# The next head's queries and key scores: in five parts between the row sums instead of in one block

## The reference, cut to what matters

```
def peer_ffn(xm, w_query, sub_keys, expert_u, expert_v):      # blocks of 128 tokens
    def one_block(xblk):
        q = (xblk @ w_query).reshape(B, TOKEN_BLOCK, N_PEER_HEADS, 2, SUBKEY_DIM)   # 8 heads, 2 x 256
        s = jnp.einsum('bthpd,hpnd->bthpn', q, sub_keys)                            # 2 x 128 key scores
        vals, idx = lax.top_k(s, PEER_TOPK)                                         # 16 of each half
        ...                                          # 256 sums, the best 16 of them, their softmax g
        u = expert_u[eidx]
        h = jnp.einsum('btd,bthkd->bthk', xblk, u)
        act = jax.nn.gelu(h, approximate=False) * g
        return jnp.einsum('bthk,bthkd->btd', act, expert_v[eidx])
```

## Time and profile before

| | us |
|---|---|
| median of 3 runs | 3779.18 (3777.73 to 3786.63) |
| the profiled execution | 3777.06 |
| its span, from the first to the last instruction | 3775.3 |
| expert stage of the first layer, first to last gather | 298 to 1065 |
| expert stage of the second layer, first to last gather | 1342 to 2104 |

### The profile page before, as it was taken

One profiled execution on the slowest core, in us unless ns is written; L12 is line 12 of the kernel. 1 busy time (PEld: TensorE's weight loads), 2 busy tenths in 40 slices (PEclk: granted clock), 3 DMA queues, 4 the chain that ended last, 5 costly groups with the idle time before them and its releaser, 6 DMA issues. The chain is left out here.

```text
span 3775.3 us, 50620 instructions
## 1 busy us (share of the span) xinstructions
PE 3284.1 (87%) x18912; PEld 2562.1 (68%) x18912; DVE 2393.1 (63%) x4688; ACT 1438.5 (38%) x2831; POOL 1237.1 (33%) x1160
## 2 busy tenths in 40 slices
PE   6997787888779878888887799999999999999999
PEld 5883343333259843443332599888899998898899
DVE  7766655655567566666655565866565656757565
ACT  4532222222146322222221344565554444655443
POOL 1306677777723067777777200000000000000000
PEclk8999999999999999999999999999999999999999
DMA  7668999999976489999999554434355554334355
GB/s 276 228 221 335 359 368 358 374 362 339 370 290 212 148 329 369 378 369 372 370 344 358 219 183 147 146 114 138 129 174 184 179 180 140 134 125 133 129 184 162
DMA packets 258289, 937.13 MB, mean 248 GB/s; under 512 B 29312, under 2 KB 30720, under 8 KB 257792
## 3 DMA queue, kind: packets, MB, share of 16 engines
q0 software_dynamic: 161280, 587.27, 41.6%
q1 hardware_dynamic: 96768, 346.62, 27.2%
HBM read 932.73 MB, written 1.05 MB: 247 GB/s over the span
## 5 line engine op out<-in xcount | busy, mean ns | idle before, releaser
L639 PE MATMUL M<-rows,diag 128*128 128x512 f32 x2048 | 1010.1, 635 | 327.0 <-DMA rows<-in_expert_v_dram,expert 210.2
L639 PEld LDWEIGHTS M<-rows,diag 128*128 128x128 f32 x2048 | 382.6, 199 | 944.1 <-issue 501.6
L252 DVE TENSOR_TENSOR w_low<-ring,w_high 128x1024 fp32r<-128x1024 f32 x560 | 688.6, 1232 | 427.4 <-ACT w_high L244 424.5
L1118 DVE CUSTOM_DVE_ANT_0 rows<-rows,attn 128x1024 f32<-128x1024 f32 x512 | 611.5, 1224 | 337.4 <-DMA rows<-in_expert_u_dram,expert 335.6
L271 PE MATMUL G<-x_high,w_high 128*128 128x256 f32 x2576 | 761.9, 296 | 60.3 <-DVE w_low L252 27.2
L274 PE MATMUL G<-x_high,w_low 128*128 128x256 f32 x2576 | 735.4, 285 | 0.0
L244 ACT ACTIVATE w_high<-ring 128x1024 fp32r<-128x1024 f32 x560 | 588.5, 1054 | 352.1 <-PE G L271 326.7
L273 PE MATMUL G<-x_low,w_high 128*128 128x256 f32 x2448 | 700.0, 286 | 0.0
L397 POOL DMA_INDIRECT rows<-in_expert_u_dram,expert x512 | 561.5, 1097 | 392.7 <-DVE expert L1100 163.6
L397 POOL DMA_INDIRECT rows<-in_expert_v_dram,expert x512 | 579.8, 1132 | 159.9 <-issue 110.7
L271 PEld LDWEIGHTS G<-x_high,w_high 128*128 128x128 f32 x2576 | 501.6, 195 | 74.5 <-issue 48.9
(11 more groups left out here) (350 smaller groups left out, 4507.2 us busy)
## 6 DMA issues: line engine op xcount, KB each, us to landing
ring<-in_stream_dram SPq DMA_DIRECT2D x654, 512.0 KB, 3.4
ada_ring<-in_ada_stream_dram POOLq DMA_DIRECT2D x80, 512.0 KB, 4.9
rows<-in_ada_stream_dram POOLq DMA_DIRECT2D x16, 512.0 KB, 17.1
rows<-in_expert_u_dram,expert POOLq DMA_INDIRECT x512, 6.2
rows<-in_expert_v_dram,expert POOLq DMA_INDIRECT x512, 6.3
const<-in_const_dram SPq DMA_DIRECT2D x1, 1096.5 KB, 11.0
x<-in_x_dram SPq DMA_DIRECT2D x1, 1024.0 KB, 5.3
out_dram<-x SPq DMA_DIRECT2D x8, 128.0 KB, 3.6
```

The costliest lines, as they stand in the source:

```text
L252: dve.tensor_tensor(T["w_low"][:, part, :], T["ring"][:, place.slot(chunk, slots), :], T["w_high"][:, part, :].bitcast(F32), ALU.subtract) ...
L639: mm = pe.matmul(M[:, 2 * t + half, :], T["diag"][:, n % 4, :], T["v_rows"][:, n % SLOTS, half * 512:(half + 1) * 512], start=(h == 0 and ...
L1118: dve.tensor_tensor_reduce(row, row, T["x_tok"][:, t, :], 1.0, 0.0, ALU.mult, ALU.add, T["hid"][:, r, k:k + 1]).then_inc(sem["u_used"], 1)
```

## The change

The function `queries` becomes a loop over five parts: parts 0 to 3 are one projection each, part 4 is the wait for the copies and the key scores. Within the expert stage nobody calls `queries` any more. On PE, part j of head h + 2 follows the row sum of one expert of head h: by (tile, expert) parts 0 and 1 behind (0, 5) and (0, 11), parts 2, 3 and 4 behind (1, 1), (1, 7) and (1, 12). On ACT the copies stand behind groups of four diagonals: by (tile, group) copies 0 and 1 behind (0, 2) and (0, 3), copies 2, 3 and 4 behind (1, 1), (1, 2) and (1, 3). The last of them stand ahead of `expert_softmax(r + 2)`. DVE, POOL and SP keep their orders, and no instruction is added or taken away.

```
+QUERY_AFTER = {(0, 5): 0, (0, 11): 1, (1, 1): 2, (1, 7): 3, (1, 12): 4}
+QUERY_COPIES = {(0, 2): 0, (0, 3): 1, (1, 1): 2, (1, 2): 3, (1, 3): 4}
...
             def queries(h):
+                for j in range(5):
+                    query_part(h, j)
+
+            def query_part(h, j):
                 g = g_peer(h)
-                for j in range(4):
-                    project(g + j, lambda k: xm[:, k, :], KD)
-                for j in range(4):
-                    evacuated(pe, g_free, g + j)
+                if j < 4:
+                    return project(g + j, lambda k: xm[:, k, :], KD)
+                for i in range(4):
+                    evacuated(pe, g_free, g + i)
...
                     mm.then_inc(sem["v_used"], 1)
+                    if h + 2 < PEER_HEADS and (t, k) in QUERY_AFTER:
+                        query_part(h + 2, QUERY_AFTER[t, k])
...
                     add_experts(h * TT + t)
-                if h + 2 < PEER_HEADS:
-                    queries(h + 2)
...
                     diagonals(at)
+                    turn = (r % TT, at % TOPK // SUB)
+                    if r // TT + 2 < PEER_HEADS and turn in QUERY_COPIES:
+                        query_part(r // TT + 2, QUERY_COPIES[turn])
...
                     expert_softmax(r + 2)
-                if r % TT == TT - 1 and r // TT + 2 < PEER_HEADS:
-                    queries(r // TT + 2)
```

More of the change, by code:

```diff
@@ L825, in queries, with query_part @@
             def queries(h):
[L826 to L829, removed]
+                for j in range(5):
+                    query_part(h, j)
+            def query_part(h, j):
+                if j < 4:
+                    copy_out(g_peer(h) + j, T["query"][:, h % 2, j, :])
+                else:
+                    copy_out(g_peer(h) + 4, T["key_score"][:, h, :], 4 * P)
             def expert_softmax(r):
```

## The result

The changed kernel takes 3680.4 us (median, 3678.3 to 3685.3) against 3781.3: ratio 0.9739, interval 0.9722 to 0.9756. The profiled execution has a span of 3676.5 us. The forecast was 3724 with a range from 3700 to 3770: the direction is right, the gain of 99 us (from the 3779.2 that the forecast started from) is nearly twice the 55 I gave.

What follows compares the result with a forecast made beforehand. The prediction took POOL's gather issues, with DMA close behind, to bound the expert stages. 3777.1 - 67 (blocks) + 12 (loads) = 3722; that execution lies 2.1 us under the median, so 3724 us, range 3700 to 3770.

Steps and rivals of the forecast that it cites:

- What bounds the stage: Expert stages: POOL issues a gather in 1.24 us at best, DMA takes 1.28 us for it; no other engine is near.
- The block's price: Query block at a head's end makes POOL stand for DVE's hid: 5.6 us by rounds, 6.1 by waits, 12 blocks.
- PE's and ACT's new waits: Parts and copies within the rounds: PE's 7 and 9.0 us fit its idle time, copies are covered; counted as nothing.
- The loads: Weight chunks loaded among the gathers: between nothing and 5.8 us a head; taken as 0.5 us a round, 12 us.
- The floor: Rounds that begin behind a block, 51.4 us, come down to the ordinary round without a block, mean 45.8 us.
- more than the block's price: Rival: POOL's issues get faster without DVE's long row of products behind the block; 3705 us; under 3700 had 0.05.
- The low end: Forecast's fastest case: 6 us beyond the forecast for faster issues and 74 us of stand given back: 3705 us.
- The loads on the path: Rival: DMA becomes the bound, 70 us against 67 gained, 3782; half gives 3747; chances 0.09 for no change, 0.15 for 3745-3768.
- PE's lateness: Rival: PE late at expert 7 of tile 1 rounds holds copy 3, ACT and DVE; +41 us, 3820; chance 0.07.

Runs made afterwards that it cites:

- after_half: The changed kernel with DVE's product taking 512 of the 1024 columns; 3636.0 us, ratio 0.9615.
- after_small: The changed kernel with each of the 21 ring chunks per layer loaded within the expert stage bringing 64 of 1024 columns; 3702.0 us, ratio 0.9787.
- after_thin: The changed kernel with projections cut to 2 of 8 matmuls and key scores to 4 of 8 within the stage; 3682.3 us, ratio 0.9740.
- after_double: The changed kernel with each of the 21 chunks per layer loaded within the stage loaded twice, one behind the other; 3726.4 us, ratio 0.9857.
- before_defer: The kernel before with only ACT's copies moved, behind the next round's first two groups of diagonals; PE's block stays whole; 3702.9 us, ratio 0.9785.

## Why the prediction was wrong, point by point

**What bounds the stage: right.** POOL's issues and DMA side by side, nothing else near. after_half shows both faces: DMA alone where loads are under way, and a fall by 4.2 us a round where they aren't.

**The block's price: right in its cause, low in size.** I chose the smaller of two numbers, 12 x 5.6 = 67 by the rounds, over 73.7 by the waits. after_small, which has no stand and nearly no loads, gains 78. That is 11 of the 44 us by which the forecast was off.

**PE's and ACT's new waits: right.** I counted them as nothing, after_thin confirms it. ACT does wait at copy 3, but it is done with it 6.3 us ahead of the next gelu:

```profile
1463.87 0.40 ACT L859 ACTIVATE diag<-const,weight 128x128 f32<-128x128 f32 x1 [0.77 <-PE M L646]
1467.33 0.39 ACT L699 ACTIVATE query<-G 128x256 f32<-128x256 f32 x1 [3.05 <-PE G L490]
1474.05 0.20 ACT L852 ACTIVATE gelu<-hid 128x4 f32<-128x4 f32 x1 [6.34 <-DVE hid L1130]
```

**The loads: the step that failed.** I wrote "so I lean to the lower end and take 0.5 us for a round, 24 rounds, 12 us", with nothing as the lower bound. The bound was one-sided. The term is 22 us of gain (3702.0 to 3680.4) for moving 15/16 of these loads, and the 34 us from my cost to this gain make up the rest of the error. I took POOL's issues as given and asked only what a load adds to DMA. But their slow part, 5.5 us a round in after_small, is 4.2 with the loads there. I had the row that shows what is at stake, an issue of 1.99 us beside DVE's products, and priced no change in it. The backlog that I used to argue that a load does no harm is there, and longer than before: a gather's time to landing is 7.8 us in the middle after, and 6.2 and 6.3 before.

```profile
rows<-in_expert_u_dram,expert POOLq DMA_INDIRECT x512, 7.8
rows<-in_expert_v_dram,expert POOLq DMA_INDIRECT x512, 7.8
```

**The floor: wrong, for the same reason.** I took the ordinary round, 45.8 us, as what a round comes down to. It held over 5 us of slow issues and was short of DMA's pace, at 386 to 353 GB/s. My own head total of 88 us for "bound by DMA" stood under the rival "more than the block's price". Its mechanism, issues that get faster, is what came, and I gave under 3700 a chance of 0.05 because most slow issues are in the ordinary rounds too; they got shorter there as well. Rounds 2 to 9 of the second layer now take 88.8 for two. The low end was not added up cleanly either: 3705 is 3779 less the 74 us of stand alone, and the 6 us for faster issues aren't in it.

**The rivals.** The loads on the path: not from the kernel before, but after_double shows its price from there on, 46 of 54 us. PE's lateness: not seen, before_defer shows a mild form of it.

**What stays open.** Why POOL's issues start later within DVE's products when loads are under way, and why they don't in before_defer, which has the same loads in bursts, no stand, and 120.2 us of slow issues.

## What to carry to other kernels

Split the time of an engine that sets the pace into three: the number of its instructions times the shortest, what they take above that, and its waits. An engine that hardly waits can't be helped by a backlog behind it, only by shorter instructions, and a change elsewhere can make them shorter or longer: here the 0.94 us issue beside a product. A stretch without the suspected stall isn't a floor; compare its rate with the best rate that the trace shows anywhere (409 GB/s here) and use that as the second bound. And a term whose sign isn't excluded by a row needs a bound on both sides of nothing.

## What the runs showed of the hardware

- In this kernel on one core, gathers and loads together run at 409 GB/s for round after round, the gathers issued by POOL at 1.24 us for 0.524 MB at best. The Trainium skill, page HBM Reference, section Specifications (TRN2), gives 358 GB/s as a core's share of its pair and says that a core alone gets more; the second holds here.
- POOL's issue of a gather takes 0.94 us. One that starts while DVE's two-input product of 1024 columns is under way stands until 0.13 us before the product's end and takes up to 1.99 us; one that starts outside a product isn't slowed by products that start behind it. With 512 columns the time above 0.94 us falls from 4.2 to 0.8 us a round (after_half). The Trainium skill, page SBUF — State Buffer, section Who interferes with whom, has a DVE instruction with two SBUF inputs contend with a GpSimd instruction that reads SBUF; a gather takes its row numbers from the tile `expert`. The runs agree in kind; whether the reading of the numbers or the making of the descriptors is held up, none of them shows.
